# Expert weights in longer runs and pairs of slots, and the bias products placed beside the fetch's third block

## The chip, the cores and the metric

One core of a Trainium2 chip runs the whole program. The metric is the device time of one execution in microseconds. TensorE (PE) does the matrix products, ScalarE (ACT) and VectorE (DVE) copy and combine, GpSimd (POOL) does a few copies, and SyncE (SP) issues most DMAs. SBUF holds the operands, PSUM the products.

## The reference, cut to what matters

One inference step of a decoder of one layer: attention for 256 prompt tokens and 64 sample tokens, then a mixture of experts, all in float32. The change is in the mixture:

```python
logits = x2d @ w_router + b_router          # 320 tokens x 32 experts
top_vals, top_idx = lax.top_k(logits, 4)
gates = softmax(top_vals)
# for each expert e, on the rows xb of its tokens:
gu = xb @ w_gate_up[e] + b_gate_up[e]       # [rows, 1024] x [1024, 2048]
g, u = gu[:, :1024], gu[:, 1024:]
g = minimum(g, 7.0); u = clip(u, -7.0, 7.0)
hid = (u + 1.0) * (g * sigmoid(1.702 * g))
out = hid @ w_down[e] + b_down[e]           # [rows, 1024] x [1024, 1024]
y[token] += gate * out
```

w_gate_up is 8 MB and w_down 4 MB per expert, so 32 experts read 402 MB.

## The kernel before

The first 400 us are projection, attention, output projection and router. Then comes the expert loop. Its unit is an *item*: one expert with up to 64 of its tokens. There are 32 experts, and an expert with more than 64 tokens gets a further item; with these inputs there are 33 items. Item 0 is written out (`body(0, first=True)`), the others run in a loop.

**Weights.** The ring has 12 slots of 1 MB: slots 0 to 7 hold w_gate_up of one expert (128 rows of 8 KB each), slots 8 to 11 hold w_down (two groups of 128 rows of 4 KB each, so a partition gets two separate runs of 4 KB). SP issues one transfer per slot (L271), each after a wait until the last item of the expert before has used the slot (`w_used`, one semaphore per slot). PE waits for `w_loaded` of a slot before its products. The weights of expert 1's w_down go to spare buffers first and are copied to the slots by POOL.

**An item on PE, in order** (`body`, L2084): the gate-up products, k = 0 to 7, one slot each, four products of 128x64 by 512 columns (L2094; two column halves run together); after k = 2 the first part of the item before is scattered into the output rows (`scatter_rows(0)`, L2076); then the turns of the next item's rows (`turn`, L1480); `scatter_rows(1)`; the fetch of the rows of the item after that (`fetch`, L1473: for each of three blocks of tokens, 128, 128 and 64, a 0/1 matrix times the block, two column halves, all summed in PSUM bank 2); the bias of the next item's gate-up (`add_bias`, L1487: a row of ones, one partition, times the bias row, one partition, into banks 0 and 1); the turns of hid (L2125); `scatter_rows(2)`, which writes banks 7 and 2; the down products (L2141), k = 0 to 7, two to a slot.

**Around it.** DVE clamps gate and up once the last k is done (L2287, L2288), which also frees banks 0 and 1 for the bias; ACT applies the sigmoid, copies the fetched rows out of bank 2 (`copy_rows`, L2167, released by `fetched`) and tells it with `xg_ready`. PE waits for `xg_ready` at L2122, ahead of the turns of hid, since bank 2 is written again by `scatter_rows(2)`. ACT also copies the turned hid (L2199, which the down products wait for) and the down products (L2203), and loads the next bias rows (`load_bias`).

All orders are written out by hand; the queues of SP and ACT run in program order.

Of the kernel before, what the change touches and what calls it, by code (L numbers as in the profile page):

```python
# [18 lines left out]
P = 128  # L19
D = 1024  # L20
# [23 lines left out]
X_BANKS = ((0, 1), (2, 3), (4, 6))  # L44
PARTS, FIRST = 30, 22
# [101 lines left out]
def decoder_step(nc, a, out, consts):  # L147
# [4 lines left out]
    with ExitStack() as ctx:  # L152
# [105 lines left out]
        def weights_of(e, s, spare=None):  # L258

            if s < KD:  # L260
                src = a["w_gate_up"][0, bass.ds(e, 1), s * P:(s + 1) * P, :].rearrange("e p n -> (e p) n")
                dst = slot[s]
            else:
                j = s - KD
                src = a["w_down"][0, bass.ds(e, 1), 2 * j * P:(2 * j + 2) * P, :].rearrange("e (r p) n -> p (e r) n", p=P)
                dst = (slot[s] if spare is None else spare).rearrange("p (r n) -> p r n", r=2)
            return dst, src
# [92 lines left out]
        with nc.Block() as block:  # L360
            @block.sync
            def _(sp):
# [91 lines left out]
                load_weights(sp, 0, 1)  # L454
# [5 lines left out]
                load_weights(sp, 0, 5)  # L460
                sp.wait_ge(mixed, N_UNITS - 1)
                load_weights(sp, 0, 2)
                load_weights(sp, 0, 3)
                sp.wait_ge(mixed, N_UNITS)
                load_weights(sp, 0, 6)
                load_weights(sp, 0, 7)
# [1010 lines left out]
        def turn_rows():  # L1477

            for c in range(4):
                ins = nc.tensor.transpose(psum[:, 2, c * P:(c + 1) * P], xg[:, c * P:(c + 1) * P], ident)  # L1480
            ins.then_inc(xg_turned, 1)

        def add_bias():

            for h in range(2):
                for n in range(2):
                    ins = nc.tensor.matmul(psum[64 * h:64 * h + 64, n, :], ones_rows[32 * n:32 * n + 1, :],  # L1487
                                           bias_row[32 * n:32 * n + 1, h * 512:h * 512 + 512],
                                           start=True, stop=False)
            ins.then_inc(bias_used, 1)  # L1490
# [13 lines left out]
        with nc.Block() as block:  # L1504
            @block.sync
            def _(sp):
# [11 lines left out]
                for n in range(2):  # L1518
                    sp.dma_start(bias_row[32 * n:32 * n + 1, :], a["b_gate_up"][0, 0:1, n * D:n * D + D]).then_inc(bias_loaded, 16)
# [463 lines left out]
        with nc.Block() as block:  # L1983
            @block.sync
            def _(sp):
# [10 lines left out]
                for s in range(KD):  # L1996
                    sp.wait_ge(w_used[s], done)
                    load_weights(sp, 1, s)
# [7 lines left out]
                with sp.Fori(2, EXPERTS) as e:  # L2006

                    done = sp.value_load(first_i[0:1, bass.ds(e, 1)], min_val=1, max_val=EXPERTS + MAX_EXTRA)  # L2008
                    for s in range(RING):
                        sp.wait_ge(w_used[s], done)  # L2010
                        load_weights(sp, e, s)
# [10 lines left out]
            def _(pe):  # L2022
# [6 lines left out]
                def fetch(t):  # L2029

                    pe.wait_ge(pick_ready, 3 * t + 3)
                    for b in range(3):
                        ins = fetch_block(b, first=(b == 0), last=(b == 2))
                    ins.then_inc(fetched, 1)
# [49 lines left out]
                def body(t, first=False):  # L2084
# [3 lines left out]
                    for k in range(KD):  # L2088
                        pe.wait_ge(w_loaded[k], loaded)
# [6 lines left out]
                        ins.then_inc(w_used[k], 1)  # L2096
# [5 lines left out]
                        if k == 2 and first:  # L2102
                            fetch(1)
# [13 lines left out]
                    fetch(t + 2)  # L2117
# [3 lines left out]
                    add_bias()  # L2121
                    pe.wait_ge(xg_ready, t + 3)  # L2122
                    pe.wait_ge(hid_ready, t + 1)
                    for c in range(4):
                        ins = nc.tensor.transpose(psum[:, 3, c * P:(c + 1) * P], hid[:, c * P:(c + 1) * P], ident)  # L2125
# [37 lines left out]
            def _(act):  # L2163
# [5 lines left out]
                def load_bias(t):  # L2169
                    e = act.value_load(expert_i[0:1, bass.ds(t, 1)], min_val=0, max_val=EXPERTS - 1)  # L2170
                    for n in range(2):
                        act.dma_start(bias_row[32 * n:32 * n + 1, :], a["b_gate_up"][0, bass.ds(e, 1), n * D:n * D + D]
# [55 lines left out]
            def _(dve):  # L2228
# [46 lines left out]
                def body(t, first=False):  # L2275
# [10 lines left out]
                    dve.wait_ge(w_used[KD - 1], t + 1)  # L2286
# [103 lines left out]
```

## Time and profile before

| | |
|---|---|
| runs | 1388.69, 1394.33, 1396.81 us, median 1394.33 |
| span of the profiled execution | 1390.1 us (its own time isn't given beside the span) |
| PE busy | 1331.7 us, 96% |
| DVE, ACT, POOL busy | 448.6, 262.0, 86.1 us |
| granted TensorE clock, mean | 0.978 |
| HBM read | 493.60 MB, 358 GB/s over the span |
| w_gate_up | 256 transfers of 1024 KB, median 18.4 us from issue to landing |
| w_down | 128 transfers of 1024 KB, 16.8 us |

The page's busy share of PE is an average over stages with different limits, and modelled at the ends of products. In the timeline a row is a group of instructions: its start, its length, engine and line, operation, what it writes and reads, the part of the array (rows x columns) and the shape, the count, and in brackets how long the engine was idle before it and what ended that. PEld is the load of the stationary operand, which runs beside the products.

### The profile page before, as it was taken

The page shows a single profiled execution, that of the slowest core. Times are in us where ns is not written, and L with a number is a line of the kernel's source. Part 1 is how long each engine was busy: PE and PEld are TensorE (multiplying, and loading weights), DVE is VectorE, ACT ScalarE, POOL GpSimd, SP SyncE. Part 2 cuts the span into 40 slices and gives each one's busy share as a digit, 9 for nine tenths or more (in the row PEclk, how much of TensorE's full clock was granted, in tenths as well). Part 3 has the DMA queues.
Part 4 walks back from the last instruction along what each step waited for, and adds up shares of the span by engine and source line. Part 5 has one row for each costly group of instructions (what it writes and reads, how often), then busy time and mean ns, then how long its engine had stood idle before and what let it go on. Part 6 is the DMA issues. An engine that isn't in the chain of part 4 may idle for free.

```text
span 1390.1 us, 20690 instructions
## 1 busy us (share of the span) xinstructions
PE 1331.7 (96%) x7774; PEld 511.9 (37%) x7775; DVE 448.6 (32%) x947; ACT 262.0 (19%) x613; POOL 86.1 (6%) x91
## 2 busy tenths in 40 slices
PE   8899998989999999999999999999999999999995
PEld 6355444554533333333333223333333333333221
DVE  1244454655662222222222232222322223222224
ACT  1332334754141101011010011000111001101002
POOL 2022233310002000000000000000000000000000
PEclk9999998997999999999999999999999999999998
DMA  9569589787078999999999998799999999999993
GB/s 361 220 233 354 199 329 363 279 315 258 28 307 332 392 418 416 417 418 418 418 418 418 417 418 359 288 418 419 418 418 418 417 416 417 419 419 418 418 416 116
DMA packets 97093, 498.42 MB, mean 359 GB/s; under 512 B 9869, under 2 KB 11021, under 8 KB 62234
## 3 DMA queue, kind: packets, MB, share of 16 engines
q1 hardware_dynamic: 85398, 430.44, 76.5%
q0 software_dynamic: 11520, 67.11, 12.5%
q8 instruction: 29, 0.48, 0.1%
q10 hardware_dynamic: 132, 0.27, 0.1%
q14 instruction: 14, 0.11, 0.0%
HBM read 493.60 MB, written 3.93 MB: 358 GB/s over the span
## 4 chain that ended last, share of the span: by engine, by line
PE 52%; DMA 9%; SPq 7%; ACT 1%; issue 1%; DVE 0%; ACTq 0%; DVEq 0%
PE psum L2094 24%; PE psum L2141 14%; DMA arena<-in_w_gate_up 9%; SPq L271 7%; PE psum L1473 6%; PE psum L2076 4%; PE psum L1487 2%; PE psum L2125 1%; PE psum L1480 1%; ACT arena L2199 1%; DVE arena L2343 0%; PE psum L2043 0%; SPq L2008 0%; PE psum L2062 0%; DVE arena L2318 0%
## 5 line engine op out<-in xcount | busy, mean ns | idle before, releaser
L2094 PE MATMUL psum<-arena 128*64 128x512 f32 x2112 | 470.9, 595 | 10.2 <-DMA arena<-in_w_gate_up 9.6
L2094 PEld LDWEIGHTS psum<-arena 128*64 128x64 f32 x2112 | 146.5, 137 | 323.5 <-issue 289.9
L2240 DVE SCALAR_TENSOR_TENSOR arena<-psum,arena 128x256 f32<-128x256 f32 (+1 forms) x128 | 110.0, 880 | 456.5 <-PE psum L2076 363.0
L2141 PE MATMUL psum<-arena 128*64 128x512 f32 x1056 | 235.4, 598 | 3.0
L2141 PEld LDWEIGHTS psum<-arena 128*64 128x64 f32 x1056 | 73.5, 138 | 151.0 <-issue 133.4
L2177 ACT ACTIVATE arena<-psum 128x512 f32<-128x512 f32 x33 | 19.7, 597 | 490.6 <-PE psum L1480 490.6
L2287 DVE TENSOR_SCALAR arena<-psum 128x512 f32<-128x512 f32 x33 | 22.8, 692 | 249.9 <-PE psum L2094 249.9
L1473 PE MATMUL psum<-arena 128*64 128x512 f32 (+1 forms) x420 | 103.1, 608 | 0.0
L1196 DVE STREAM_TRANSPOSE arena<-arena 128x1024 f32<-128x1024 f32 x64 | 74.9, 1215 | 1.8 <-DVE arena L1300 0.9
L2076 PE MATMUL psum<-arena 64*128 64x512 f32 x264 | 74.5, 641 | 0.9 <-ACT arena L2203 0.9
L583 PE MATMUL psum<-arena 128*128 128x512 f32 x128 | 63.8, 631 | 3.6 <-DVE arena L1185 3.6
L2203 ACT ACTIVATE arena<-psum 128x512 f32<-128x512 f32 x33 | 19.7, 597 | 242.4 <-PE psum L2141 242.4
L1473 PEld LDWEIGHTS psum<-arena 128*64 128x64 f32 (+1 forms) x420 | 23.9, 134 | 75.3 <-issue 73.0
L739 PE MATMUL psum<-arena 128*16 128x128 f32 x1024 | 44.0, 290 | 5.4 <-issue 5.2
L672 PE MATMUL psum<-arena 128*32 128x264 f32 x512 | 37.5, 412 | 4.7 <-issue 3.3
L2167 ACT ACTIVATE arena<-psum 128x512 f32<-128x512 f32 x34 | 20.3, 597 | 97.2 <-PE psum L1473 97.2
L1487 PE MATMUL psum<-arena 1*64 1x512 f32 x272 | 37.9, 626 | 0.0
L583 PEld LDWEIGHTS psum<-arena 128*128 128x128 f32 x128 | 23.3, 198 | 28.4 <-issue 23.0
L254 POOL DMA_INDIRECT arena<-in_cache_diff_v,small_i x32 | 30.3, 948 | 51.9 <-PE psum L745 44.3
L739 PEld LDWEIGHTS psum<-arena 128*16 128x16 f32 x1024 | 27.0, 101 | 15.5 <-issue 12.6
L571 PE MATMUL psum<-arena 128*128 128x256 f32 x128 | 31.5, 401 | 0.8 <-ACT arena L878 0.8
L2076 PEld LDWEIGHTS psum<-arena 64*128 64x128 f32 x264 | 19.9, 184 | 33.4 <-issue 33.4
(268 smaller groups left out, 1027.0 us busy)
## 6 DMA issues: line engine op xcount, KB each, us to landing
arena<-in_w_gate_up SPq DMA_DIRECT2D x256, 1024.0 KB, 18.4
arena<-in_w_down SPq DMA_DIRECT2D x128, 1024.0 KB, 16.8
arena<-in_w_in SPq DMA_DIRECT2D x12, 1024.0 KB, 24.2
arena<-in_w_out SPq DMA_DIRECT2D x4, 1024.0 KB, 9.8
arena<-in_x_prompt SPq DMA_DIRECT2D x4, 512.0 KB, 4.8
out<-arena SPq DMA_DIRECT2D x8, 256.0 KB, 2.1
arena<-in_b_gate_up ACTq DMA_DIRECT2D x66, 4.0 KB
arena<-in_ln_g SPq DMA_DIRECT2D x2, 512.0 KB, 6.8
```

The costliest lines, as they stand in the source:

```text
L271: sp.dma_start(*weights_of(e, s)).then_inc(w_loaded[s], 16)
L571: ins = nc.tensor.matmul(psum[:, bank, PROMPT * (part // 2):PROMPT * (part // 2 + 1)], w[:, m * P:(m + 1) * P], xT[:, k, 0:PROMPT], start= ...
L583: ins = nc.tensor.matmul(psum[:, bank, :], xT[:, k, b * P:(b + 1) * P], w, start=(k == 0), stop=(k == KD - 1))
L672: ins = nc.tensor.matmul(z_of(u, h)[32 * g:32 * g + 32, :], q_blocks[u % 2][:, j, :], T[:, j, :], start=(y == 0 and d == 0), stop=(y == 1 ...
L739: nc.tensor.matmul(psum[32 * g:32 * g + 16, O_BANK, 0:P], w_past[n][:, r:r + 16], V_raw[buf(u)][:, pg * 512 + g * P:pg * 512 + (g + 1) * P ...
L1196: ins = nc.vector.transpose(turned[:, :, :, d, :], raw[:, :, :, 2 * h + d, :])
L1473: ins = nc.tensor.matmul(psum[64 * h:64 * h + 64, 2, :], pick_rows[0:nt, b, :], x1[0:nt, b, h * 512:(h + 1) * 512], start=first, stop=last)
L1487: ins = nc.tensor.matmul(psum[64 * h:64 * h + 64, n, :], ones_rows[32 * n:32 * n + 1, :], bias_row[32 * n:32 * n + 1, h * 512:h * 512 + 51 ...
L2076: ins = nc.tensor.matmul(psum[:, banks[h], :], scatter[r, t0:t0 + nt], y_rows[r, :], start=True, stop=True)
L2094: ins = nc.tensor.matmul(psum[64 * h:64 * h + 64, n, :], x_k, slot[k][:, col:col + 512], start=False, stop=(k == KD - 1))
L2141: ins = nc.tensor.matmul(psum[64 * h:64 * h + 64, 4, :], h_k, slot[s][:, col:col + 512], start=(k == 0), stop=(k == KD - 1))
L2240: ins = nc.vector.scalar_tensor_tensor(out=rows, in0=products, scalar=item_gate[:, b, col], in1=rows, op0=ALU.mult, op1=ALU.add)
```

## The change

Three things are changed. (1) Layout: a partition now gets two neighbouring rows of a block of 256, so w_down comes in runs of 8 KB and w_gate_up in transfers of 2 MB with runs of 16 KB into two slots at once. The turns of the rows and of hid read with a step of two floats to match. (2) Waits in pairs: for slots 0 to 7 SP waits for and loads only the even ones, PE waits at even k and releases at odd k, on the even slot's semaphore. (3) The bias rows go to partitions 64 and 96, and the fetch is split: the two blocks of 128 tokens as before, then the bias products, then the third block of 64 tokens, which lies on partitions 0 to 63. `fetched` is raised by the third block, as before.

```diff
@@ -42,6 +42,7 @@
 X_BANKS = ((0, 1), (2, 3), (4, 6))
+BIAS_AT = (64, 96)
 PARTS, FIRST = 30, 22
@@ -258,12 +259,12 @@
             if s < KD:
-                src = a["w_gate_up"][0, bass.ds(e, 1), s * P:(s + 1) * P, :].rearrange("e p n -> (e p) n")
-                dst = slot[s]
+                src = a["w_gate_up"][0, bass.ds(e, 1), s * P:(s + 2) * P, :].rearrange("e (p r) n -> (e p) (r n)", r=2)
+                dst = ring[:, s * SLOT:(s + 2) * SLOT]
             else:
                 j = s - KD
-                src = a["w_down"][0, bass.ds(e, 1), 2 * j * P:(2 * j + 2) * P, :].rearrange("e (r p) n -> p (e r) n", p=P)
-                dst = (slot[s] if spare is None else spare).rearrange("p (r n) -> p r n", r=2)
+                src = a["w_down"][0, bass.ds(e, 1), 2 * j * P:(2 * j + 2) * P, :].rearrange("e (p r) n -> (e p) (r n)", r=2)
+                dst = slot[s] if spare is None else spare
             return dst, src
@@ -451,19 +452,15 @@
                 load_weights(sp, 0, 0)
-                load_weights(sp, 0, 1)
                 sp.wait_ge(mixed, N_UNITS - 2)
...
                 load_weights(sp, 0, 4)
-                load_weights(sp, 0, 5)
                 sp.wait_ge(mixed, N_UNITS - 1)
                 load_weights(sp, 0, 2)
-                load_weights(sp, 0, 3)
                 sp.wait_ge(mixed, N_UNITS)
                 load_weights(sp, 0, 6)
-                load_weights(sp, 0, 7)
                 sp.wait_ge(key_rows_out, 4 * 16)
@@ -1476,16 +1473,17 @@
 
+            pairs = xg.rearrange("p (j q r) -> p j r q", j=2, r=2)
             for c in range(4):
-                ins = nc.tensor.transpose(psum[:, 2, c * P:(c + 1) * P], xg[:, c * P:(c + 1) * P], ident)
+                ins = nc.tensor.transpose(psum[:, 2, c * P:(c + 1) * P], pairs[:, c // 2, c % 2, :], ident)
             ins.then_inc(xg_turned, 1)
...
                 for n in range(2):
-                    ins = nc.tensor.matmul(psum[64 * h:64 * h + 64, n, :], ones_rows[32 * n:32 * n + 1, :],
-                                           bias_row[32 * n:32 * n + 1, h * 512:h * 512 + 512],
+                    ins = nc.tensor.matmul(psum[64 * h:64 * h + 64, n, :], ones_rows[BIAS_AT[n]:BIAS_AT[n] + 1, :],
+                                           bias_row[BIAS_AT[n]:BIAS_AT[n] + 1, h * 512:h * 512 + 512],
                                            start=True, stop=False)
@@ -1516,7 +1514,7 @@
                 for n in range(2):
-                    sp.dma_start(bias_row[32 * n:32 * n + 1, :], a["b_gate_up"][0, 0:1, n * D:n * D + D]).then_inc(bias_loaded, 16)
+                    sp.dma_start(bias_row[BIAS_AT[n]:BIAS_AT[n] + 1, :], a["b_gate_up"][0, 0:1, n * D:n * D + D]).then_inc(bias_loaded, 16)
                 for s in range(8, RING):
@@ -1993,7 +1991,7 @@
                 done = sp.value_load(first_i[0:1, 1:2], min_val=1, max_val=EXPERTS + MAX_EXTRA)
-                for s in range(KD):
+                for s in range(0, KD, 2):
                     sp.wait_ge(w_used[s], done)
@@ -2006,7 +2004,7 @@
                     done = sp.value_load(first_i[0:1, bass.ds(e, 1)], min_val=1, max_val=EXPERTS + MAX_EXTRA)
-                    for s in range(RING):
+                    for s in (0, 2, 4, 6, 8, 9, 10, 11):
                         sp.wait_ge(w_used[s], done)
@@ -2026,12 +2024,15 @@
 
-                def fetch(t):
+                def fetch_prompt(t):
 
                     pe.wait_ge(pick_ready, 3 * t + 3)
-                    for b in range(3):
-                        ins = fetch_block(b, first=(b == 0), last=(b == 2))
-                    ins.then_inc(fetched, 1)
+                    for b in range(2):
+                        fetch_block(b, first=(b == 0), last=False)
+
+                def fetch_samples():
+
+                    fetch_block(2, first=False, last=True).then_inc(fetched, 1)
 
@@ -2086,21 +2087,24 @@
                     for k in range(KD):
-                        pe.wait_ge(w_loaded[k], loaded)
+                        if k % 2 == 0:
+                            pe.wait_ge(w_loaded[k], loaded)
                         x_k = xgT[:, (k % 4) * P + (k // 4) * 64:(k % 4) * P + (k // 4) * 64 + 64]
...
                                                        start=False, stop=(k == KD - 1))
-                        ins.then_inc(w_used[k], 1)
+                        if k % 2:
+                            ins.then_inc(w_used[k - 1], 1)
                         if k == 2 and not first:
...
                         if k == 2 and first:
-                            fetch(1)
+                            fetch_prompt(1)
+                            fetch_samples()
                         if k == 5 and first:
@@ -2114,15 +2118,17 @@
                     pe.wait_ge(xg_copied, t + 2)
-                    fetch(t + 2)
+                    fetch_prompt(t + 2)
                     pe.wait_ge(gate_clamped, t + 1)
...
                     add_bias()
+                    fetch_samples()
                     pe.wait_ge(xg_ready, t + 3)
                     pe.wait_ge(hid_ready, t + 1)
+                    pairs = hid.rearrange("p (j q r) -> p j r q", j=2, r=2)
                     for c in range(4):
-                        ins = nc.tensor.transpose(psum[:, 3, c * P:(c + 1) * P], hid[:, c * P:(c + 1) * P], ident)
+                        ins = nc.tensor.transpose(psum[:, 3, c * P:(c + 1) * P], pairs[:, c // 2, c % 2, :], ident)
                     ins.then_inc(hid_turned, 1)
@@ -2169,7 +2175,7 @@
                     for n in range(2):
-                        act.dma_start(bias_row[32 * n:32 * n + 1, :], a["b_gate_up"][0, bass.ds(e, 1), n * D:n * D + D]
+                        act.dma_start(bias_row[BIAS_AT[n]:BIAS_AT[n] + 1, :], a["b_gate_up"][0, bass.ds(e, 1), n * D:n * D + D]
                                       ).then_inc(bias_loaded, 16)
@@ -2283,7 +2289,7 @@
                         drain(0, bass.ds(t - 1, 1), PART[0]).then_inc(drained, 1)
-                    dve.wait_ge(w_used[KD - 1], t + 1)
+                    dve.wait_ge(w_used[KD - 2], t + 1)
                     nc.vector.tensor_scalar(gate_in, psum[:, 0, :], LIMIT, None, ALU.min).then_inc(gate_clamped, 1)
...
                     dve.wait_ge(gate_clamped, t + 1)
```

## Rows read from the trace of the kernel before

**Rows 1.** The page: busy time of PE; shares of the chain by engine.

```profile
PE 1331.7 (96%) x7774; PEld 511.9 (37%) x7775; DVE 448.6 (32%) x947; ACT 262.0 (19%) x613; POOL 86.1 (6%) x91
...
PE 52%; DMA 9%; SPq 7%; ACT 1%; issue 1%; DVE 0%; ACTq 0%; DVEq 0%
```

**Rows 2.** Chain of waits in order of time (start us, us, what), fetch products alone.

```profile
452.44 2.88 PE psum L1473 x12
...
740.90 2.88 PE psum L1473 x12
...
861.81 2.88 PE psum L1473 x12
...
1179.12 2.88 PE psum L1473 x12
...
1238.85 2.88 PE psum L1473 x12
...
1360.63 2.88 PE psum L1473 x12
```

**Rows 3.** Timeline of PE, 1190 to 1330: products of the last slot.

```profile
1265.71 1.94 PE L2094 MATMUL psum<-arena 128*64 128x512 f32 x8 [0.56 <-DMA arena<-in_w_gate_up]
```

**Rows 4.** SP's timeline, 760 to 1390; window 868:872 (engines' busy, PEclk, DMA share, GB/s).

```profile
875.96 13.56 SPq L271 DMA_DIRECT2D arena<-in_w_gate_up  x8
...
868.00:872.00 4.00, 4.00 (x22) 1.33 (x20) 1.11 (x6) 0.00 (x0) 0.00 (x0) 1.00 0.00 0
```

**Rows 5.** DMA queues in windows 615.5:621.5, 597:607, 100.5:102.1, 190.5:192.5.

```profile
DMA packets 631, 2.45 MB, mean 408 GB/s; under 512 B 33, under 2 KB 33, under 8 KB 631
q1 hardware_dynamic: 631, 2.45, 102.2%
...
DMA packets 580, 4.23 MB, mean 423 GB/s; under 512 B 64, under 2 KB 64, under 8 KB 64
q1 hardware_dynamic: 580, 4.23, 101.6%
...
q0 software_dynamic: 40, 0.66, 95.5%
...
q0 software_dynamic: 46, 0.75, 95.6%
```

**Rows 6.** Groups of PE by shape, 370 to 400: turns with a step, and plain.

```profile
L1560 PE MATMUL psum<-arena 128*128 128x128 f32 x8 | 1.3, 286 | 0.0
...
L1480 PE MATMUL psum<-arena 128*128 128x128 f32 x4 | 0.7, 287 | 0.0
```

**Rows 7.** Timeline of one item between fetch and down products.

```profile
654.77 0.14 PEld L1473 LDWEIGHTS psum<-arena 128*64 128x64 f32 x2 [0.29 <-issue]
...
656.16 0.20 PEld L1473 LDWEIGHTS psum<-arena 64*64 64x64 f32 x4 [0.81 <-issue]
657.17 0.21 PEld L1487 LDWEIGHTS psum<-arena 1*64 1x64 f32 x8 [0.81 <-issue]
...
657.28 0.60 ACT L2167 ACTIVATE arena<-psum 128x512 f32<-128x512 f32 x1 [2.83 <-PE psum L1473]
658.18 0.42 PEld L2125 LDWEIGHTS psum<-arena 128*128 128x128 f32 x4 [0.81 <-ACT arena L2167]
...
658.88 0.60 ACT L2199 ACTIVATE arena<-psum 128x512 f32<-128x512 f32 x1 [1.00 <-PE psum L2125]
659.53 0.20 PEld L2141 LDWEIGHTS psum<-arena 128*64 128x64 f32 x4 [0.55 <-ACT arena L2199]
```

**Rows 8.** Timeline of the weight loads, 200.6 to 201.6.

```profile
200.57 0.24 PEld L739 LDWEIGHTS psum<-arena 128*16 128x16 f32 x8
201.03 0.13 PEld L745 LDWEIGHTS psum<-arena 8*16 8x16 f32 x8 [0.21 <-issue]
201.37 0.30 PEld L667 LDWEIGHTS psum<-arena 128*128 128x128 f32 x2 [0.21 <-issue]
```

**Rows 9.** Line 745 alone: idle before it (us, times).

```profile
  issue: 3.6, 16
```

## The prediction

> **What bounds the kernel now.** I read the page first. TensorE (PE) is busy 96% of the span, yet the chain of waits gives it only 52% and hands the rest to DMA, to the sync queue and to PE's other lines [rows 1]. Two resources are nearly level, so the next view has to say which one ends each stretch: the chain of waits in order of time. The fetch products (L1473) run once per item, so their start times are a clock of the expert loop. From 452.44 to 740.90 there are 10 items, from 861.81 to 1179.12 eleven: 28.85 us each in both stretches. From 740.90 to 861.81 four items take 120.91, 5.5 more than 4 x 28.85. From 1179.12 to 1360.63 six take 181.51, 8.4 more. In the last four, from 1238.85, an item costs 30.445 us [rows 2]. There PE stops before the products of a slot until that slot's w_gate_up has landed [rows 3]. So PE's own item is 28.85 us, the DMA engines need 30.44 us for an expert's 12 MB, and the DMA falls 1.6 us behind per item until it has used up a lead; only then does it set the time. Eleven PE-paced items times 1.6 make a lead of about 17.5 us. The lead is won back once, in the middle, where one expert has two items and holds the ring: w_gate_up is issued only from 875.96 on, with the DMA engines idle before it [rows 4]. What DMA costs today is thus 5.5 + 8.4 = 14 us, not 1.6 us times 32.
>
> **The change part by part.**
>
> *Longer runs.* Three windows hold nearly one size of run each. 4 KB (w_down): 102.2% of 16 engines x 6 us over 631 - 33 = 598 runs is 0.164 us per run. 8 KB (w_gate_up): 101.6% x 16 x 10 us over 516 is 0.315 us. So 4 KB more cost 0.151, and 0.013 is a fixed part per run. 16 KB runs are in the trace on the software queue alone: 95.5% x 16 x 1.6 us over 40 is 0.611 us in one window and 95.6% x 16 x 2 us over 46 is 0.665 in another, amid other traffic [rows 5]. An engine now moves 64 runs of 4 KB and 64 of 8 KB per expert: 64 x (0.164 + 0.315) = 30.7, against 30.44 in the chain, a factor of 0.993. After the change it moves 32 of 8 KB and 32 of 16 KB: 32 x (0.315 + 0.611) x 0.993 = 29.4 us. With 0.617 (linear from the two hardware sizes) it is 29.6; I take 29.5. With 0.665 it would be 31.1, and that end I keep for the range. At 29.5 the DMA stays 0.65 us behind an unchanged PE item, 11 us in the 17 items after the middle, under the lead of 17.5: the 14 us go. What is late next is PE itself, from the first item to the last.
>
> *Waiting and releasing in pairs.* One step of k is 8 products, 1.9 us [rows 3]. Release comes one step later for the even slot, use needs the odd slot one step earlier: the lead shrinks by about 3.8 us to 13.7, still over 11. While PE sets the pace this costs nothing; were DMA the bound, it would cost up to 3.8 us once at the end. The SP queue issues four gate-up transfers instead of eight and has nothing else behind them but w_down of the same expert, whose slots are released later anyway. Below zero: four waits fewer per item on PE, which had long been satisfied, so nothing.
>
> *Strided transposes.* hid and xg are turned with a step of two floats. The router's turns (L1560) already read with a step of four: 286 ns each, against 287 for the plain ones [rows 6]. Cost 0; at most, if only that line were lucky, some 0.1 us per turn.
>
> *Bias products beside the third block.* This is the step that decides. Now an item runs, by the weight loads: third block of the fetch at 656.16, bias at 657.17, turns of hid at 658.18: 1.01 us each. ACT copies the fetched rows at 657.28 for 0.60 us, and the turns wait for that copy too (xg_ready, L2122); it ends at 657.88 and is hidden by the bias products [rows 7]. After the change the bias comes first and the copy starts only behind the third block. The cover is gone. If bias and third block run one after the other, the bias starts at 656.16, the block at 657.17, it ends at 658.18, the copy runs from 658.29 to 658.89, and the turns load 0.05 later (that is the distance from L2199's end, 659.48, to L2141's load at 659.53): 658.95 instead of 658.18. That is +0.77 us. All behind it (hid turns, scatter, copy of hidT, down products) moves with it, since each waits for the one before. If they run together, both end near 657.2, the copy runs to 657.93 and the turns load at 657.98: -0.20 us.
>
> Do they run together? They use different rows of the array (0-63 against 64 and 96), so nothing collides. But they are of different shapes, 1x64 and 64x64. The trace never shows two such groups on disjoint rows. What it does show: a weight load of the same shape as the running products is drawn ahead (0.29 us of idle between the loads in a run of L1473), while each load of a new shape comes only after 0.81 us of idle, when the products have run out [rows 7]. The nearest case to disjoint tiles is the attention's: four column groups of 128x16, then four of 8x16. The first of the new loads goes to column group 0, free since its own product was over, and with a spare weight buffer that the same shape would have used. It still waits 0.21 us, just as the 128x128 load behind it does, which needs the whole array [rows 8]; over the 16 such places 3.6 us [rows 9]. So a change of shape waits for the whole array. I take +0.77.
>
> The Trainium skill has the rule in "TensorEngine Tiling (Array Packing)", section "Key Properties": changing the tiling mode, not just the tile, drains TensorE. By it the sum is the slower one. Against it stands "TensorE: Matmul & The Clock Gate", section "The mechanism": a load for a row group that doesn't conflict is pulled ahead of running products. By that it would be the faster one. The trace agrees with the first as far as it goes; no run here has shown a disjoint pair yet.
>
> *The sum.* Span 1390.1; minus 14.0 for DMA; plus 33 items x 0.77 = 25.4: 1401.5. PE's item is then 29.62 us, over the DMA's 29.5, so the lead isn't touched at all. The page gives no time beside the span; the median of the runs, 1394.33, lies 4.2 over it, and I carry that over: **1405.7 us**, slower by 0.8%.
>
> **The rivals.**
>
> 1. *The shapes do overlap*, and it is faster. PE's item becomes 28.65: 1390.1 - 14.0 - 6.6 = 1369.5. DMA at 29.5 then falls behind by 0.85 x 17 = 14.5 against a lead of 13.7, so about 1 us comes back: with 4.2, 1375 us. For it: the bias products at rows 0 and 32 and both column halves already run four at once, 8 instructions in 1.01 us, the time of two. Against it: the waits at each change of shape above. The side is decided by what the turns lose: with the 14 us gained, the break-even is 14 / 33 = 0.42 us per item.
>
> 2. *Runs of 16 KB are no faster on the hardware queue*, and the shapes overlap. Then only w_down gains, 32 x (2 x 0.164 - 0.315) = 0.4 us per expert, or nothing, and the end is DMA's: the 14 us stay or half of them go, the pairs cost up to 3.8: 1388 to 1398, no change. For it: no hardware transfer before has runs over 8 KB.
>
> 3. *Half the cost*: a change of shape waits for the rows it needs only in part, the turns lose some 0.35 us: 1390.1 - 14.0 + 11.6 + 4.2 = 1392, no change.
>
> 4. *The 16 KB runs are slower* (31.1 us per expert) beside the slower PE: DMA then falls behind by 1.5 us per item, nearly as now, and takes back 10 us or so: about 1415.
>
> **How the numbers follow.** Forecast 0.52, with its own range 1401 to 1411 (0.1 us per item is 3.3 us; the shown runs spread by 8 us). Rival 1: 0.33. Rival 2: 0.08. Rival 3: 0.04. Rival 4: 0.03. A measurement can tell about 0.5%, 7 us. Faster by more: 0.33. Within: 0.12. Slower: 0.55. As two cases of opposite sign hold most of it, the range has to reach from the one to the other: 1373 to 1411.
>
> **What would show it.** In the profile after: no product of L2094 waits for w_gate_up; gate-up transfers of 2 MB; the DMA has pauses instead of a share over 1 everywhere. The weight load of the third block about 1.0 us behind that of the bias (forecast) or within 0.1 us (rival 1); the turns of hid led by a wait on ACT of about 0.77 us; an L1473 cadence of 29.6 us (forecast), 28.65 (rival 1) or 30.4 in the last items (rival 2). The prediction is wrong if the two groups' products overlap, or if the turns start without waiting for the copy.

## The result and the profile after

The changed kernel takes 1441.58 us (median of 4 runs, 1440.74 to 1449.33) where the kernel before takes 1395.57 on the same chip: a ratio of 1.0349, 95% interval 1.0319 to 1.0378. It is slower, as forecast, but by 3.5% where 0.8% was said, and 30 us above the end of the range. The span of the profiled execution went from 1390.1 to 1438.9 us. The runs of the changed kernel take 1.8 us more than their spans (1440.74 and 1438.9); the 4.2 us that the forecast added was the difference between two executions, not this.

The page of the kernel after, busy time, chain by engine and issues of the weights:

```profile
PE 1367.5 (95%) x7774; PEld 529.1 (37%) x7775; DVE 448.8 (31%) x947; ACT 262.3 (18%) x613; POOL 86.4 (6%) x91
...
PE 69%; ACT 2%; DVE 0%; DMA 0%; issue 0%; ACTq 0%; DVEq 0%
...
arena<-in_w_gate_up SPq DMA_DIRECT2D x128, 2048.0 KB, 11.4
arena<-in_w_down SPq DMA_DIRECT2D x128, 1024.0 KB, 7.6
```

DMA is out of the chain (9% before, [rows 1]) and ACT has come in. PE's busy time grew by 36 us although it executes the same 7774 products: the same work took longer. That is the first thing to see.

One item of the kernel after, from the timeline, answers to [rows 7]:

```profile
673.15 0.21 PEld L1485 LDWEIGHTS psum<-arena 1*64 1x64 f32 x8 [0.81 <-issue]
674.16 0.19 PEld L1470 LDWEIGHTS psum<-arena 64*64 64x64 f32 x4 [0.81 <-issue]
675.29 0.60 ACT L2173 ACTIVATE arena<-psum 128x512 f32<-128x512 f32 x1 [3.85 <-PE psum L1470]
675.94 0.55 PEld L2131 LDWEIGHTS psum<-arena 128*128 128x128 f32 x4 [1.58 <-ACT arena L2173]
676.61 0.21 PEld L2081 LDWEIGHTS psum<-arena 64*64 64x64 f32 x8
677.37 0.20 PEld L2147 LDWEIGHTS psum<-arena 128*64 128x64 f32 x4 [0.55 <-ACT arena L2205]
```

The third block's weights (L1470, 64*64) load 1.01 us after those of the bias (L1485): nothing overlaps. ACT's copy starts 1.13 us after that load, and the turns of hid (L2131) load at 675.94, 2.79 us behind the bias, where before they came 2.02 us behind the third block: +0.77, to the digit. The copy's place on the path is as forecast. But the four turns now take 0.67 us to the next load (675.94 to 676.61) against 0.59 before.

The start of the fetch in five neighbouring items, from the chain of waits:

```profile
1254.03 1.87 PE psum L1470 x8
1285.24 1.87 PE psum L1470 x8
1316.40 1.87 PE psum L1470 x8
1346.19 1.87 PE psum L1470 x8
1377.40 1.87 PE psum L1470 x8
```

The items take 31.21, 31.16, 29.79 and 31.21 us. Before, all that weren't held up by DMA took 28.85 [rows 2]. Two things happen: every item is longer by 0.94, and two in three by 1.4 more. Windows over two stretches of the kernel after (us, busy of PE, PEld, DVE, ACT, POOL, granted clock, DMA share, GB/s) and the timeline of PE show what the 1.4 is:

```profile
659.75:689.54 29.79, 29.00 (x142) 9.53 (x141) 7.20 (x14) 2.91 (x5) 0.00 (x0) 1.00 1.00 418
...
645.00:648.30 3.30, 3.30 (x16) 1.41 (x18) 1.07 (x3) 0.60 (x1) 0.00 (x0) 0.51 1.06 452
```

```profile
644.86 1.13 PE L2131 MATMUL psum<-arena 128*128 128x128 f32 x4 [0.70 <-ACT arena L2173]
645.91 1.13 PE L2081 MATMUL psum<-arena 64*64 64x256 f32 x8
646.97 7.70 PE L2147 MATMUL psum<-arena 128*64 128x512 f32 x32
```

The granted clock falls to 0.51, that is to the lower of TensorE's two levels, 1.2 GHz in place of 2.4, from about the end of PE's wait for the copy until some 3.3 us later. In that stretch the turns take 1.13 us instead of 0.74, the scatter 1.13 instead of 0.66, the down products 7.70 instead of 7.09. Ahead of it stand the fetch, the bias and the third block, each with a drain between them, and the 0.70 us in which PE waits for ScalarE. In the expert loop of the kernel before the clock is 1.00 in each 100 us from 500 to 1300, though PE is idle there too. The first line below is of the kernel before, the second of the kernel after:

```profile
1200.00:1300.00 100.00, 96.17 (x460) 29.70 (x458) 23.44 (x45) 9.84 (x17) 0.00 (x0) 1.00 1.02 417
...
1200.00:1300.00 100.00, 97.81 (x456) 31.62 (x456) 23.66 (x50) 8.88 (x16) 0.00 (x0) 0.96 0.99 403
```

The kernel before idles more, 3.8 us in 100 against 2.2, and keeps its clock. Its gaps of 0.2 to 0.6 us, waits for w_gate_up, stand between products of one shape; the gap of 0.70 us after the change stands where one shape follows another. So the amount of idle time alone doesn't tell whether the clock falls.

**Where the 48.8 us of span come from.** 31 items at 29.79 instead of 28.85: +29.1. The 20 of them with a fall of the clock: +27.5 (the cadences of the chain less 29.79 each). The first cadence of the loop, 37.25 instead of 31.40: +5.9; there the bias products also wait for their own DMA, which the chain of the changed kernel has at 418.32 for 5.64 us. The last item: +0.8. DMA's waits are gone: -13.9. Sum +49.4, and the stretch ahead of the loop gives back 0.7.

### The profile page after: what moved, and what is told of

Same layout as the page of the kernel before. It is cut to its first block, busy times and chain, and to the rows that moved or that the text cites. A ratio compares the mean times of both kernels' runs of the same rounds, so it can differ in the third digit from the quotient of the medians.

```text
span 1438.9 us, 20322 instructions
## 1 busy us (share of the span) xinstructions
PE 1367.5 (95%) x7774; PEld 529.1 (37%) x7775; DVE 448.8 (31%) x947; ACT 262.3 (18%) x613; POOL 86.4 (6%) x91
## 4 chain that ended last, share of the span: by engine, by line
PE 69%; ACT 2%; DVE 0%; DMA 0%; issue 0%; ACTq 0%; DVEq 0%
PE psum L2096 32%; PE psum L2147 18%; PE psum L1470 7%; PE psum L2077 5%; PE psum L1485 2%; PE psum L2131 2%; PE psum L2081 2%; PE psum L1478 1%; ACT arena L2173 1%; ACT arena L2205 1%; DMA arena<-in_b_gate_up 0%; DVE arena L2349 0%; PE psum L2044 0%; PE psum L2063 0%; DVE arena L2324 0%
## 5 line engine op out<-in xcount | busy, mean ns | idle before, releaser
L2096 PE MATMUL psum<-arena 128*64 128x512 f32 x2112 | 466.5, 594 | 0.6 <-PEq L1502 0.6
L2096 PEld LDWEIGHTS psum<-arena 128*64 128x64 f32 x2112 | 148.0, 137 | 308.1 <-issue 306.5
L2147 PE MATMUL psum<-arena 128*64 128x512 f32 x1056 | 253.9, 636 | 1.1
L2147 PEld LDWEIGHTS psum<-arena 128*64 128x64 f32 x1056 | 77.2, 148 | 170.1 <-issue 148.4
L1470 PE MATMUL psum<-arena 128*64 128x512 f32 (+1 forms) x420 | 105.4, 608 | 0.0
L1470 PEld LDWEIGHTS psum<-arena 128*64 128x64 f32 (+1 forms) x420 | 24.0, 134 | 75.5 <-issue 72.9
L2131 PE MATMUL psum<-arena 128*128 128x128 f32 x132 | 29.2, 356 | 23.0 <-ACT arena L2173 23.0
L2131 PEld LDWEIGHTS psum<-arena 128*128 128x128 f32 x132 | 20.3, 210 | 52.1 <-ACT arena L2173 52.1
L1485 PE MATMUL psum<-arena 1*64 1x512 f32 x272 | 37.5, 621 | 1.9 <-DMA arena<-in_b_gate_up 1.9
L580 PEld LDWEIGHTS psum<-arena 128*128 128x128 f32 x128 | 22.5, 191 | 27.0 <-issue 21.5
```

Source lines behind the costliest of these rows:

```text
L580: ins = nc.tensor.matmul(psum[:, bank, :], xT[:, k, b * P:(b + 1) * P], w, start=(k == 0), stop=(k == KD - 1))
L1470: ins = nc.tensor.matmul(psum[64 * h:64 * h + 64, 2, :], pick_rows[0:nt, b, :], x1[0:nt, b, h * 512:(h + 1) * 512], start=first, stop=last)
L2096: ins = nc.tensor.matmul(psum[64 * h:64 * h + 64, n, :], x_k, slot[k][:, col:col + 512], start=False, stop=(k == KD - 1))
L2131: ins = nc.tensor.transpose(psum[:, 3, c * P:(c + 1) * P], pairs[:, c // 2, c % 2, :], ident)
L2147: ins = nc.tensor.matmul(psum[64 * h:64 * h + 64, 4, :], h_k, slot[s][:, col:col + 512], start=(k == 0), stop=(k == KD - 1))
```

## The experiments

The kernels below ran on three other chips, on which the kernel before takes 1380.1, 1380.3 and 1381.3 us; each ratio is to the kernel before on the same chip, and items are compared by the cadence of the fetch in the chain or the timeline.

**The order turned round.** The whole fetch first, then the bias.

```diff
                     fetch_prompt(t + 2)
+                    fetch_samples()
                     pe.wait_ge(gate_clamped, t + 1)
                     pe.wait_ge(e_dve, 2 * t + 1)
                     pe.wait_ge(bias_loaded, 32 * t + 64)
                     add_bias()
-                    fetch_samples()
```

> The changed kernel with one step turned round: the whole fetch first, then the bias products (still on partitions 64 and 96), so that ScalarE's copy is covered again. Theory (the shapes drain the array and the uncovered copy opens a gap of 0.77 us, after which the clock falls in two items of three): item 28.85 plus 0.18 for the two strided turns, 29.03 us, no clock fall in the loop, DMA at 29.5 per expert: span about 1380 to 1386, faster than before by 0.5 to 1%. Rival A (the long runs or pairs are what costs the time): it stays at 1430 or above. Rival B (bias on 64/96 itself matters): the item stays at 29.8 or the clock still falls, 1410 to 1440.

Measured: 1374.69 us, ratio 0.9961 (0.9950 to 0.9973). The timeline of PE has the cadence 29.02, no fall of the clock after the first item, and DMA's pace in the last one only (29.94):

```profile
1255.65 2.94 PE L1470 MATMUL psum<-arena 128*64 128x512 f32 x12
1284.67 2.94 PE L1470 MATMUL psum<-arena 128*64 128x512 f32 x12
1313.89 2.94 PE L1470 MATMUL psum<-arena 128*64 128x512 f32 x12
1343.83 2.94 PE L1470 MATMUL psum<-arena 128*64 128x512 f32 x12
```

Moving one line takes the whole loss away. The long runs, the pairs and the partitions of the bias are all still there, so together they don't cost it. The gain over before, 0.4%, is a little under the 0.5 to 1% expected: the item is as expected, 0.17 longer, but the first cadence (33.86) is 2.5 us longer, and that wasn't in the sum.

**The bias rows back on partitions 0 and 32**, order kept.

```diff
-BIAS_AT = (64, 96)
+BIAS_AT = (0, 32)
```

> The changed kernel with the bias rows back on partitions 0 and 32, where they share the rows of the third block, and the changed order kept. Theory (a change of shape drains the array wherever the tiles lie): nothing changes, items of 29.79, 31.2, 31.2 and 1441 us within 0.3%. Rival (disjoint rows did overlap in part, only hidden by something else): slower than the changed kernel by up to 1 us per item, 33 us.

Measured: 1428.70 us, ratio 1.0358 (1.0339 to 1.0376), with items of 29.79, 31.21 and 31.16, as the changed kernel (whose ratio is 1.0349; the 1441 us expected were of another chip). The timeline of the weight loads:

```profile
659.51 0.21 PEld L1485 LDWEIGHTS psum<-arena 1*64 1x64 f32 x8 [0.81 <-issue]
660.53 0.20 PEld L1470 LDWEIGHTS psum<-arena 64*64 64x64 f32 x4 [0.81 <-issue]
662.30 0.55 PEld L2131 LDWEIGHTS psum<-arena 128*128 128x128 f32 x4 [1.58 <-ACT arena L2173]
```

On the rows that the third block uses too, the bias is 1.02 us ahead of it; on free rows it was 1.01. Placing it beside the block bought nothing.

**The bias part alone**, on the kernel before: partitions 64 and 96 and the new order, single slots, old runs.

```diff
-                    fetch(t + 2)
+                    fetch_prompt(t + 2)
...
                     add_bias()
+                    fetch_samples()
```

> The kernel before with only the bias part of the change (partitions 64 and 96, bias ahead of the third block), weights in the old runs and single slots. Theory: item 28.85 + 0.77 = 29.62; if the clock falls because of the gap alone, it falls here as well, in about as many items: 1430 +- 8 us. If the clock's fall needs the DMA or the strided part of the change, only the drain shows: 1400 to 1405.

Measured: 1428.82 us, ratio 1.0362 (1.0340 to 1.0384). Items of 29.61 us (28.85 + 0.76), and of 30.9 to 31.1 with a fall of the clock; 23 of the 31 items have one. So the clock's fall needs neither the DMA part nor the step in the turns, and the whole loss sits in the bias part. The 14 us of DMA's waits go here too, for the plain reason that PE at 30.7 on average is slower than the old DMA at 30.44.

**Work in the gap.** The changed kernel with one product more, whose result nobody uses.

```diff
                     fetch_samples()
+                    nc.tensor.matmul(psum[:, 4, 0:320], ident, tab[:, 0:320], start=True, stop=True)
                     pe.wait_ge(xg_ready, t + 3)
```

> The changed kernel with one product more (128x128 by 320 columns, result unused) in the gap behind the third block, so that PE works while it waits for ScalarE's copy. Theory (the gap of 0.77 us costs twice, itself and by the clock that falls after it): items of 29.8 us all through, no clock fall, span 1438.9 - 22 x 1.4 = about 1408, slower than before by 1%. Rival (the clock falls for another reason, the DMA or the long stretch of small products): items still 29.8, 31.2, 31.2, and 1440 or more.

Measured: 1401.89 us, ratio 1.0166 (1.0148 to 1.0184). Timeline, then the chain:

```profile
657.38 0.20 PEld L1470 LDWEIGHTS psum<-arena 64*64 64x64 f32 x4 [0.81 <-issue]
658.39 0.81 PE L2127 MATMUL psum<-arena 128*128 128x320 f32 x2
658.50 0.60 ACT L2174 ACTIVATE arena<-psum 128x512 f32<-128x512 f32 x1 [3.84 <-PE psum L1470]
659.15 0.55 PEld L2132 LDWEIGHTS psum<-arena 128*128 128x128 f32 x4 [0.47 <-ACT arena L2174]
```

```profile
982.22 1.87 PE psum L1470 x8
1012.00 1.87 PE psum L1470 x8
1041.79 1.87 PE psum L1470 x8
```

Every item takes 29.79 us and the clock doesn't fall once after the loop's first item. The critical path is the same: the turns still wait for the copy. 26.9 us less (1428.7 to 1401.9, by the run with the bias rows on 0 and 32 on the same chip) is what the falls of the clock took, and what a useless product gives back; 31 us were expected. The rest, 22 us over before, is the path: 31 items at +0.94, the first cadence (36.98 instead of 31.40, +5.6) and the last item (+0.9), less the 14 us of DMA. This is the run that splits the loss in two.

**The wait moved** behind the turns, in front of a small product.

```diff
-                    pe.wait_ge(xg_ready, t + 3)
                     pe.wait_ge(hid_ready, t + 1)
...
                     ins.then_inc(hid_turned, 1)
+                    pe.wait_ge(xg_ready, t + 3)
+                    nc.tensor.matmul(psum[:, 4, 0:8], ident, tab[:, 0:8], start=True, stop=True)
```

> The changed kernel with the wait for ScalarE's copy moved behind the turns of hid, in front of a product of 128x128 by 8 columns (result unused) and the third scatter, the only one that writes the copied bank. Theory (the cost is the wait on PE's path, doubled by the clock): the turns start about 1.0 us after the third block's load, as before the change; what is left of the gap lies between turns and scatter, 0.1 to 0.3 us; items of 29.2 to 29.5 us, clock falls few or none; slower than before by 0 to 0.7%. Rival (the clock falls from the row of small products, not from the gap): items still 31 in two of three.

Measured: 1401.20 us, ratio 1.0157 (1.0135 to 1.0179): slower by 1.6% where 0 to 0.7% was expected. The item without a fall is 29.26, as expected, 0.53 less than the changed kernel's, but the clock falls 11 times in the loop, in three items of eight. Timeline:

```profile
715.51 0.74 PE L2130 MATMUL psum<-arena 128*128 128x128 f32 x4
716.28 0.39 PE L2133 MATMUL psum<-arena 128*128 128x8 f32 x2
716.59 0.21 PEld L2081 LDWEIGHTS psum<-arena 64*64 64x64 f32 x8
```

PE has hardly a gap here. So the wait for the copy isn't needed for a fall: the rival is true in part. The kernel before had shown the same once, in its own first item in the loop. From 419.32 PE goes without a gap through turns, scatter, fetch, bias, turns and scatter, with a change of shape from each to the next, and then the clock falls (a window as above):

```profile
426.80:430.10 3.30, 3.30 (x16) 0.97 (x10) 2.37 (x6) 0.00 (x0) 0.00 (x0) 0.51 1.01 408
```

The forecast didn't price it.

**The step moved to the writers**, with the old order.

```diff
-            pairs = xg.rearrange("p (j q r) -> p j r q", j=2, r=2)
...
-                nc.scalar.activation(xg, psum[:, 2, :], ACT.Copy)
+                nc.scalar.activation(parted(xg), by_pairs(psum[:, 2, :]), ACT.Copy)
...
-                    nc.vector.tensor_tensor(hid, up_in, sig, ALU.mult)
+                    nc.vector.tensor_tensor(parted(hid), by_pairs(up_in), by_pairs(sig), ALU.mult)
```

> As e1_bias_last, and the step of two floats is moved from PE's turns to those who write the rows: ScalarE's copy and VectorE's last product read with the step and write in two halves. Theory (a turn read with a step costs PE 0.09 us, two per item): item 29.02 - 0.18 = 28.85 us, 6 us less than e1_bias_last, faster than before by 0.7 to 0.9%. Rival (ScalarE's copy takes over 0.2 us longer with the step and its cover is gone): item 29.0 or more, no gain.

Measured: 1384.47 us, ratio 1.0025 (1.0010 to 1.0040). The rival holds. Timeline:

```profile
717.36 0.21 PEld L1490 LDWEIGHTS psum<-arena 1*64 1x64 f32 x8 [0.81 <-issue]
717.48 1.07 ACT L2177 ACTIVATE arena<-psum 128x512 f32<-128x512 f32 x1 [2.83 <-PE psum L1470]
718.60 0.42 PEld L2135 LDWEIGHTS psum<-arena 128*128 128x128 f32 x4 [1.03 <-ACT arena L2177]
```

The copy takes 1.07 us in place of 0.60 with the step, outlasts the bias products and stands on the path again; the item is 29.07 and in six items in a row the clock falls (30.75); in the other 25 it doesn't. The turns are back at 0.42 of loads and 0.59 to the next: the step had cost PE 0.09 per group of four turns. Paid on ScalarE it costs more. That instruction also writes in two halves now, and no run tells reading with the step from writing in halves.

**Bias products in the third block's shape**, 64 rows (63 of them zero) by 64 columns on partitions 64 to 127, on that kernel.

```diff
+                    bias_products(0)
                     fetch_samples()
-                    add_bias()
+                    bias_products(1).then_inc(bias_used, 1)
```

This kernel and the last two also wait for the bias row (`bias_loaded`) and for VectorE ahead of the fetch, and no longer behind its second block.

> As e6_plain_turns, but the bias products get the shape of the third block: 64 rows (partitions 64 to 127, zero but for one) by 64 columns, first half of them issued ahead of the third block, second half behind it. Theory (disjoint tiles of one shape overlap, disjoint tiles of two shapes don't): the weight loads of third block and first bias follow each other within 0.1 us, block and bias together take 1.87 us in place of 2.02, the copy stays covered; item 28.70 us, 5 us less than e6_plain_turns. Rival (row halves don't overlap either in this use): three rounds of 0.86, item 29.5 or more, slower by 20 us, and clock falls.

Measured: 1380.78 us, ratio 1.0006 (0.9995 to 1.0017). The slow copy stands on the path here too (item 29.09), so the total says little. The timeline answers the question:

```profile
709.24 0.65 PE L1495 MATMUL psum<-arena 64*64 64x512 f32 x2
709.25 0.65 PE L1470 MATMUL psum<-arena 64*64 64x512 f32 x2
709.72 0.60 PE L1495 MATMUL psum<-arena 64*64 64x512 f32 x2
709.74 0.60 PE L1470 MATMUL psum<-arena 64*64 64x512 f32 x2
711.51 0.66 PE L2148 MATMUL psum<-arena 128*128 128x128 f32 x4 [0.34 <-ACT arena L2190]
```

Bias (L1495) and third block (L1470) run side by side, 0.01 us apart, their weight loads too (709.24 and 709.25). The bias still comes first and on other rows than the block; its shape is now the block's. The turns wait 0.34 us for the copy in each item, and yet the clock is 1.00 over the whole of 450 to 1350.

**w_down's runs of 8 KB alone**, on the kernel before, with hid written in halves by VectorE.

```diff
-                src = a["w_down"][...].rearrange("e (r p) n -> p (e r) n", p=P)
+                src = a["w_down"][...].rearrange("e (p r) n -> (e p) (r n)", r=2)
```

> The kernel before with only w_down's runs of 8 KB (written by VectorE in halves, so PE's turns stay plain), w_gate_up and bias as they were. Theory (DMA's 30.44 us per expert falls by 0.4 to 30.0, PE's 28.85 stays): the loop still ends on DMA after the middle, but later; of the 14 us some 7 to 9 go: faster than before by 0.5%. If the long runs of w_gate_up and the pairs bring the rest, e6_plain_turns is faster than this one by 4 to 6 us. Rival (the long w_gate_up runs bring nothing, w_down's bring all): both are level.

Measured: 1373.22 us, ratio 0.9949 (0.9931 to 0.9968), item 28.85, and where DMA sets the pace, at the end, 30.15. That is within the forecast of 7 to 9 us less (7.1). From the timeline of PE:

```profile
1281.66 2.94 PE L1473 MATMUL psum<-arena 128*64 128x512 f32 x12
1311.81 2.94 PE L1473 MATMUL psum<-arena 128*64 128x512 f32 x12
1341.98 2.94 PE L1473 MATMUL psum<-arena 128*64 128x512 f32 x12
```

One line of the three parts, without steps on PE, already has all that was gained.

**A plain copy and plain turns**, the fetch products reading the token rows with the step.

```diff
-                                       x1[0:nt, b, h * 512:(h + 1) * 512], start=first, stop=last)
+                                       x1[0:nt, b, h * 512:(h + 1) * 512].rearrange("p (j q r) -> p j r q", j=2, r=2),
+                                       start=first, stop=last)
```

> As e1_bias_last, but nothing that PE or ScalarE reads or writes alone has the step: the fetch products read the token rows with a step of two floats as their moving operand, so the fetched rows come out in the turned order, and VectorE writes hid in halves. Theory (a step costs 0.09 us in a turn and 0.47 us in ScalarE's copy, and is free in a moving operand or in VectorE's slack): item 28.85 us until DMA's 29.6 takes over near the end, 5 us less than e1_bias_last: 1368 to 1371 where before is 1380. Rival (the step slows the moving operand as well, 12 instructions per item): item above 29.0.

Measured: 1374.27 us, ratio 0.9952 (0.9939 to 0.9965). The item is 28.98, not 28.85, and the total 3 us above the expected 1368 to 1371: the step isn't free in a moving operand either. The three rounds of the fetch cost 0.13 more, two strided turns had cost 0.17.

**Everything together, in two forms.** The changed kernel with bias products in the third block's shape, between its halves, and hid written with the step by VectorE:

```diff
                     fetch_prompt(t + 2)
-                    add_bias()
+                    bias_products(0)
                     fetch_samples()
+                    bias_products(1).then_inc(bias_used, 1)
...
-                        ins = nc.tensor.transpose(psum[:, 3, c * P:(c + 1) * P], pairs[:, c // 2, c % 2, :], ident)
+                        ins = nc.tensor.transpose(psum[:, 3, c * P:(c + 1) * P], hid[:, c * P:(c + 1) * P], ident)
```

> The bias products in the third block's shape, half before and half behind it, with plain copies: the turn of the fetched rows keeps its step, VectorE writes hid in halves. Theory: 28.85 - 0.15 for the overlapped block + 0.09 for the turn = 28.79 us per item, up to the point where DMA's 29.6 us per expert ends the lead: 1368 to 1372. Rival (the copy is exposed again, as in e7_same_shape): item 29.0 or more.

In the second form the step of xg goes from the turns to the fetch products as well:

```diff
-                                       x1[0:nt, b, h * 512:(h + 1) * 512], start=first, stop=last)
+                                       x1[0:nt, b, h * 512:(h + 1) * 512].rearrange("p (j q r) -> p j r q", j=2, r=2),
+                                       start=first, stop=last)
...
-                ins = nc.tensor.transpose(psum[:, 2, c * P:(c + 1) * P], pairs[:, c // 2, c % 2, :], ident)
+                ins = nc.tensor.transpose(psum[:, 2, c * P:(c + 1) * P], xg[:, c * P:(c + 1) * P], ident)
```

> e10_plain_copy with the bias products in the third block's shape. Theory: item 28.70 us; the DMA then falls behind by 0.9 us per item against a lead of some 14, so that the last items run at 29.6 to 29.9: 1365 to 1369, faster than before by 0.8 to 1.1%, the fastest of all. Rival (DMA sets the end as soon as PE is under 28.85): level with e10_plain_copy.

Measured: 1376.89 us, ratio 0.9965 (0.9951 to 0.9979), and 1375.83, ratio 0.9964 (0.9954 to 0.9974). Both are slower than expected (1368 to 1372 and 1365 to 1369). The items are the shortest of all, 28.77 and 28.78, and the total isn't: the rival of the second (DMA sets the end) holds. Fetch starts of the second kernel at its end, from the timeline of PE:

```profile
1226.52 2.03 PE L1470 MATMUL psum<-arena 128*64 128x512 f32 x8
1256.33 2.03 PE L1470 MATMUL psum<-arena 128*64 128x512 f32 x8
1286.26 2.03 PE L1470 MATMUL psum<-arena 128*64 128x512 f32 x8
1316.14 2.03 PE L1470 MATMUL psum<-arena 128*64 128x512 f32 x8
```

29.87 on average: DMA's pace with runs of 16 KB and 8 KB, against 30.15 with 8 KB alone and 30.44 at first. The DMA queues' rate over 1250 to 1340 in this kernel, in the one with w_down alone and in the kernel before:

```profile
DMA packets 3547, 38.32 MB, mean 426 GB/s; under 512 B 403, under 2 KB 403, under 8 KB 409
```

```profile
DMA packets 5216, 37.96 MB, mean 422 GB/s; under 512 B 581, under 2 KB 581, under 8 KB 587
```

```profile
DMA packets 6706, 37.57 MB, mean 417 GB/s; under 512 B 581, under 2 KB 581, under 8 KB 3659
```

From the third fetch to the last, 31 items, the last four kernels (w_down alone, plain copy, and these two) take 900.0 to 900.2 us, whatever their PE item is; the kernel before takes 908.2. Their totals differ ahead of that. The last two wait for the first bias row ahead of the fetch, 3.87 and 3.42 us of idle PE, and their first two cadences are 52.8 and 52.4 us, against 50.9 with a plain copy and 48.3 with w_down alone.

No version tried beats the kernel before by more than 0.5%, and the simplest of those that reach it is w_down's part alone.

## Why the prediction was right and wrong, step by step

**What bounds the kernel: right.** PE's 28.85 and DMA's 30.44 are what decides, and DMA's waits did go. That they went says little for the longer runs, though: in the run with the bias part alone they went too, with the old runs, because PE had become slower. This term of the sum came out whatever the runs bring.

**A change of shape waits for the whole array: right**, and now shown for disjoint rows. Rows 64 and 96 or rows 0 and 32: 1.01 and 1.02 us between the loads; one shape: 0.01. The attention's column groups [rows 8] had pointed to it. The Trainium skill says in "TensorEngine Tiling (Array Packing)", section "Key Properties", that a change of the tiling mode, and not just of the tile, drains TensorE; the trace agrees, with 1.01 us. The Trainium skill also says in "TensorE: Matmul & The Clock Gate", section "The mechanism", that a load for a row group that doesn't conflict is pulled ahead of running products; that holds in the run with one shape (0.01 us) and not across shapes (1.01 us).

**The copy's cover is gone, +0.77: right** to 0.01 us.

**The sum: wrong.** This is the step that failed. It took the length of PE's item to be the only thing that the new order touches, and left TensorE's clock out, a term put at nothing without a reason. It is larger than the exposed copy itself: 27.5 us in the 20 items with a fall, and part of the first cadence, against 31 x 0.77 = 23.9. The run with work in the gap shows it as 26.9 us without any change to the path. The forecast treated 0.77 us of idle PE as 0.77 us of time. All rivals shared the omission, which is why the range ended 30 us short. The signs that the forecast named for being wrong, products that overlap or turns that don't wait for the copy, didn't show: its mechanism held and its time was wrong all the same. The profile before had a hint, the fall to 0.51 in the loop's first item, and a clock of 1.00 in the rest only says that the loop as it stood kept it up.

**The first cadence: left out.** It is 5.9 us longer, by the exposed copy, a wait of 1.93 us for the bias row and a longer stretch at the lower clock (10 us, 426.5 to 436.5, where before it is 3.3). The sum had it as one item like the others.

**Turns with a step cost nothing: wrong.** A group of four costs 0.09 us more, two groups per item, 5.6 us in all; the forecast's own upper value, some 0.1 us, was the one to take. [rows 6] compare the time of one product, 286 and 287 ns. The cost is in the weight loads: in the changed kernel 0.55 us for four against 0.42. The trace before had it. The router's loads with a step (L1560) take 209 ns on average, the plain ones of the turns (L1480) 140. A group is to be measured by the distance to the next group's start, as it was for the bias.

**Longer runs: half right.** 29.5 us per expert was said, 29.87 measured. No hardware transfer before had runs of 16 KB, and the value came from the software queue and the fit. The direction came out, and so nearly did the gain of w_down alone, 0.4 us per expert (30.44 to 30.15 measured, 0.3). At 29.87 DMA is slower than PE in every kernel whose item is 28.8 to 29.0, so their end is DMA's again. In the changed kernel it didn't matter, PE being slower still.

**Pairs of slots: right** as far as shown: no stall in the loop. The first cadence grew from 31.4 to 33.86 us in the kernel with the order turned round, and not in the one with w_down alone (31.35). There the bias products wait 0.59 us for their own small DMA and the clock stays low longer. That DMA takes 4.52 us in the run with the bias part alone (old runs, single slots), 5.31 with the order turned round and 5.64 in the changed kernel, so the new loads of the weights delay it by about 1 us. Whether the transfers of 2 MB or the runs of 16 KB do it stays open; it wasn't tried.

**Also open** is what exactly brings the clock down. Filling the gap stops it, so the gap matters; but neither its length nor the item's orders the runs:

| PE's item without a fall, us | PE idle before the turns of hid, us | falls in 31 items |
|---|---|---|
| 28.85 (before) | none | 0 |
| 29.07 (step moved to the writers) | 0.15 | 6 |
| 29.09 (one shape) | 0.34 | 0 |
| 29.26 (wait behind the turns) | none | 11 |
| 29.61 (bias part alone) | 0.70 | 23 |
| 29.79 (the changed kernel) | 0.70 | 20 |
| 29.79 (the gap filled) | none | 0 |

And in the kernel with the step moved to the writers, items of the same length have a fall or not.

## What to carry to other kernels

Before moving an instruction, ask what it covered, and look for the wait that was satisfied only because of it; here that was a copy of 0.6 us which a wait two lines below had never had to wait for. An idle PE costs just its length only where the clock stays up: price a new gap among products of changing shapes twice, once as time and once as a possible fall of the clock, and keep the second in the range. Here products on disjoint rows of the array ran together once they had one shape; if that is wanted, pad the smaller one to it.

## What was not expected of the hardware

A read with a step of two floats cost time wherever it was put: 0.09 us in four turns as PE's stationary operand, 0.13 in three rounds as its moving operand. With the result also written in halves it cost 0.47 in ScalarE's copy from PSUM (0.60 to 1.07) and 0.38 in VectorE's product (0.69 to 1.07), the last hidden, since VectorE had time to spare. A useless product of 0.8 us, placed in a wait, made the kernel 27 us faster.
